# Output projection and the norm behind it joined into one stage by blocks of tokens

## What is computed

```python
h = layer_norm(ALPHA * x + 0.5 * swiglu(x, ...[0]), ln_g[0], ln_b[0])
...   # h @ w_in; retention, forgetting attention and cross-attention, merged by gates g
mix = (g[:, :, 0] * ret_out + g[:, :, 1] * fox_out + g[:, :, 2] * mem_out) @ w_out
h = layer_norm(ALPHA * h + mix, ln_g[1], ln_b[1])
y = layer_norm(ALPHA * h + 0.5 * swiglu(h, w_ffn_gate[1], w_ffn_up[1], w_ffn_down[1]), ln_g[2], ln_b[2])
```

## Time and profile before

| | |
|---|---|
| median of 3 runs | 3609.65 us (3609.44 to 3610.64) |
| the profiled execution | 3616.08 us, span of the core 3614.3 us |
| mean granted TensorE clock | 0.952 of full |
| TensorE matmuls busy | 3295.3 us, 91% of the span |
| VectorE, ScalarE, GpSimd busy | 911.9, 632.3, 792.8 us |
| first load of `w_out` issued | 2565.34 us after the span's start |
| first matmul of the projection | 2577.50 |
| first matmul of the norm | 2681.60 |
| first matmul of the feed-forward layer behind | 2742.89 |

### The profile page before, as it was taken

One profiled execution on the slowest core, in us unless ns is written; L12 is line 12 of the kernel. 1 busy time (PEld: TensorE's weight loads), 2 busy tenths in 40 slices (PEclk: granted clock), 3 DMA queues, 4 the chain that ended last, 5 costly groups with the idle time before them and its releaser, 6 DMA issues. The chain is left out here.

```text
span 3614.3 us, 55597 instructions
## 1 busy us (share of the span) xinstructions
PE 3295.3 (91%) x21001; PEld 2981.3 (82%) x21001; DVE 911.9 (25%) x1606; ACT 632.3 (17%) x1179; POOL 792.8 (22%) x696
## 2 busy tenths in 40 slices
PE   5999999998797898788999899999796999999996
PEld 5999999997796798555888666666686999999995
DVE  3111111113406231555110122222323111111114
ACT  3000000001201111344100244444113000000003
POOL 0232322333120121022111111111021323232220
PEclk7999999999898899899999999999798999999998
DMA  5111111110101211211111499999201111111111
GB/s 144 32 53 37 46 46 35 52 47 24 34 25 38 58 41 56 83 57 48 36 53 38 141 307 291 300 304 302 74 23 35 41 38 49 35 49 49 33 38 54
DMA packets 328683, 293.37 MB, mean 81 GB/s; under 512 B 33641, under 2 KB 249065, under 8 KB 328049
## 3 DMA queue, kind: packets, MB, share of 16 engines
q1 hardware_dynamic: 317136, 275.93, 24.5%
q0 software_dynamic: 11424, 15.76, 1.6%
HBM read 279.34 MB, written 12.26 MB: 81 GB/s over the span
## 5 line engine op out<-in xcount | busy, mean ns | idle before, releaser
L207 PE MATMUL f_acc<-x_hi,w_hi_last 128*128 128x364 f32 x1056 | 233.3, 329 | 27.4 <-SPq L489 27.4
L165 POOL CAST w_hi_first<-w_raw_first 128x1024 fp32r<-128x1024 f32 (+1 forms) x96 | 82.7, 862 | 741.2 <-issue 301.4
L207 PE MATMUL f_acc<-x_hi,w_hi_first 128*128 128x364 f32 x1056 | 233.5, 329 | 6.9 <-SPq L489 6.9
L207 PE MATMUL f_acc<-x_hi,w_lo_first 128*128 128x364 f32 x1056 | 234.2, 330 | 0.0
L207 PE MATMUL f_acc<-x_lo,w_hi_first 128*128 128x364 f32 x1056 | 234.0, 330 | 0.0
L207 PE MATMUL f_acc<-x_hi,w_lo_last 128*128 128x364 f32 x1056 | 233.9, 330 | 0.0
L207 PE MATMUL f_acc<-x_lo,w_hi_last 128*128 128x364 f32 x1056 | 233.5, 329 | 0.0
L165 POOL CAST w_hi_last<-w_raw_last 128x1024 fp32r<-128x1024 f32 (+2 forms) x92 | 73.3, 797 | 612.4 <-PE f_acc L207 608.5
L596 DVE SCALAR_TENSOR_TENSOR br<-f_acc,br 128x1092 f32 x88 | 114.0, 1296 | 368.8 <-PE f_acc L207 368.8
L207 PEld LDWEIGHTS f_acc<-x_hi,w_hi_last 128*128 128x128 f32 x1056 | 183.9, 189 | 28.0 <-issue 28.0
L207 PEld LDWEIGHTS f_acc<-x_hi,w_hi_first 128*128 128x128 f32 x1056 | 184.0, 189 | 7.1 <-issue 7.1
(11 more groups left out here) (402 smaller groups left out, 6322.1 us busy)
## 6 DMA issues: line engine op xcount, KB each, us to landing
br<-cache_fox_k SPq DMA_DIRECT2D x256, 256.0 KB, 5.4
br<-cache_fox_v SPq DMA_DIRECT2D x256, 256.0 KB, 6.6
w_raw_first<-w_ffn_gate SPq DMA_DIRECT2D x22, 512.0 KB, 3.8
w_raw_first<-w_ffn_up SPq DMA_DIRECT2D x22, 512.0 KB, 3.8
w_raw_last<-w_ffn_gate SPq DMA_DIRECT2D x22, 512.0 KB, 3.9
w_raw_last<-w_ffn_up SPq DMA_DIRECT2D x22, 512.0 KB, 3.8
w_raw_first<-w_ffn_down SPq DMA_DIRECT2D x40, 256.0 KB, 2.8
w_raw_last<-w_ffn_down SPq DMA_DIRECT2D x40, 256.0 KB, 2.8
```

The costliest lines, as they stand in the source:

```text
L165: self.nc.gpsimd.tensor_copy(hi, raw).then_inc(self.high[s], 1)
L207: mm = self.nc.tensor.matmul(out[:, b, 0:width], w[s][:, k, :], x[:, k, b * width:(b + 1) * width], start=(k == 0 and first), stop=(k == k ...
```

## The change

`phase_out` and `phase_norm(1)` become one stage, `phase_out_norm`. The tokens are cut into blocks of 416, 416 and 260 columns. The work of the projection is 24 units, each one output tile for one block (24 matmuls, one PSUM bank out of a ring of six). Tiles 0 and 1 run together over the three blocks, then tiles 2 and 3, then tiles 4 to 7 block by block. Weights have four slots for the parts and two for the raw tiles, which lie in rows 8 and 9 of `g.br`. The parts of `mix` are made by quarters: block 0 in two halves of the channels, then block 1, then block 2. The norm is that of the class `Norm`, its steps set between units by hand: the mean of block 0 behind unit 17, its variances behind unit 19, and so on. Squares go into `mix`, the reciprocals into `mem_kt` and `mem_v`. The order on VectorE and ScalarE is written out. The first weights of the feed-forward layer are loaded at the end of SP's list and no longer split in the norm; ScalarE and VectorE split them at the start of `phase_ffn(1)`.

```diff
@@ phase_ffn
             @block.scalar
             def _(act):
+                if layer == 1:
+                    w.first_high(act, KD)
                 act.preload_act_table(ACT.Silu)
...
             @block.vector
             def _(dve):
+                if layer == 1:
+                    w.first_low(dve, KD)
+
@@ phase_out_norm, in place of phase_out and phase_norm(g, 1)
+    STARTS = [0, 416, 832, TW]
+    BLOCKS, HALF, SLOTS, BANKS = 3, KD // 2, 4, 6
+    UNITS = [(j, b) for pair in range(2) for b in range(BLOCKS) for j in (2 * pair, 2 * pair + 1)] \
+        + [(j, b) for b in range(BLOCKS) for j in range(HALF, KD)]
+    LAST = [1 + max(i for i, unit in enumerate(UNITS) if unit == (j, BLOCKS - 1)) for j in range(KD)]
+        quarters = [(0, slice(0, HALF)), (0, slice(HALF, KD))] + [(b, slice(0, KD)) for b in range(1, BLOCKS)]
...
             @block.sync
             def _(sp):
+                for j in range(KD):
+                    if j >= 2:
+                        sp.wait_ge(low, j - 1)
+                    sp.dma_start(w.raw[j % 2], io["w_out"][:, j * P:(j + 1) * P].rearrange("(k p) c -> p k c", p=P))\
+                        .then_inc(loaded[j % 2], 16)
+                sp.wait_ge(low, KD)
+                w.load_next(sp, w.n, ffn_first(io, 1), KD)
             @block.gpsimd
             def _(pool):
+                n1.constants()
+                def split(j):
+                    pool.wait_ge(loaded[j % 2], 16 * (j // 2 + 1))
+                    if j >= SLOTS:
+                        pool.wait_ge(summed, LAST[j - SLOTS])
+                    nc.gpsimd.tensor_copy(hi[j % SLOTS][:], w.raw[j % 2]).then_inc(high, 1)
+                    pool.wait_ge(high, j + 1)
+                    nc.gpsimd.tensor_tensor(lo[j % SLOTS][:], w.raw[j % 2], hi[j % SLOTS][:].bitcast(F32), ALU.subtract)\
+                        .then_inc(low, 1)
+                pool.wait_ge(low, 2)
+                for j in range(2, KD):
+                    split(j)
+                for b in range(BLOCKS):
+                    pool.wait_ge(added, 3 * HALF + HALF * (b + 1))
+                    n1.add_up(pool, b)
             @block.tensor
             def _(pe):
+                def unit(i):
+                    j, b = UNITS[i]
+                    s = j % SLOTS
+                    pe.wait_ge(low, j + 1)
+                    if i >= BANKS:
+                        pe.wait_ge(added, i - BANKS + 1)
+                    for k in range(KD):
+                        if k % HALF == 0:
+                            pe.wait_ge(mix_low, 1 + k // HALF if b == 0 else b + 2)
+                        for x, (wt, src) in enumerate(((hi, g.xh), (hi, g.xl), (lo, g.xh))):
+                            mm = nc.tensor.matmul(bank[i % BANKS][:, 0:n1.width(b)], wt[s][:, k, :], src[:, k, n1.cols(b)],
+                                                  start=(k == 0 and x == 0), stop=(k == KD - 1 and x == 2))
+                    mm.then_inc(summed, 1)
+                units(0, 18)
+                n1.means(pe, 0)
+                units(18, 20)
+                n1.variances(pe, 0)
+                units(20, 22)
+                n1.means(pe, 1)
+                units(22, 24)
+                n1.variances(pe, 1)
+                n1.means(pe, 2)
+                n1.variances(pe, 2)
             @block.scalar
             def _(act):
...
+                n1.square(act, 0)
+                n1.deviation(act, 0)
+                n1.shifted(act, 0, g.xh)
+                n1.square(act, 1)
+                n1.deviation(act, 1)
+                n1.shifted(act, 1, g.xh)
+                n1.square(act, 2)
+                n1.deviation(act, 2)
+                n1.shifted(act, 2, g.xh)
+                for b in range(BLOCKS):
+                    scaled_back(b)
             @block.vector
             def _(dve):
...
+                residual(0)
+                residual(1)
+                weight_lows(0)
+                mix_lows(0)
+                mix_lows(1)
+                weight_lows(1)
+                residual(2)
+                mix_lows(2)
+                residual(3)
+                mix_lows(3)
+                dve.wait_ge(resid, 4)
+                adds(0, 19)
+                n1.centre(dve, 0)
+                adds(19, 22)
+                n1.invert(dve, 0)
+                n1.scale(dve, 0)
+                adds(22, 23)
+                n1.centre(dve, 1)
+                adds(23, 24)
+                n1.invert(dve, 1)
+                n1.scale(dve, 1)
+                n1.centre(dve, 2)
+                lows(0)
+                n1.invert(dve, 2)
+                n1.scale(dve, 2)
+                lows(1)
+                lows(2)
```

More of the change, by code:

```diff
@@ L2814, in _, with units @@
+                def units(first, end):
+                    for i in range(first, end):
+                        unit(i)
+                pe.wait_ge(n1.ready, 2)
+                units(0, 18)
[8 more added lines that the diff above has]
+                n1.variances(pe, 2)
             @block.scalar
@@ L2815, in _ @@
             def _(act):
[L2816 to L2819, removed]
+                for j in range(2):
+                    act.wait_ge(loaded[j], 16)
+                    nc.scalar.copy(hi[j][:], w.raw[j]).then_inc(high, 1)
+                    if j == 0:
+                        for q in range(2):
+                            act.wait_ge(resid, q + 1)
+                            nc.scalar.copy(part(g.xh, q), part(mix, q)).then_inc(mix_high, 1)
@@ new lines, in _, with scaled_back @@
+                for q in range(2, 4):
+                    act.wait_ge(resid, q + 1)
+                    nc.scalar.copy(part(g.xh, q), part(mix, q)).then_inc(mix_high, 1)
+                nc.scalar.mul(alpha_b[:], n1.shift, ALPHA).then_inc(alpha_ok, 1)
+                act.wait_ge(alpha_ok, 1)
+                act.wait_ge(n1.ready, 2)
+                def scaled_back(b):
+                    for k in range(KD):
+                        act.wait_ge(low_row, b * KD + k + 1)
+                        row = g.res[:, k, n1.cols(b)]
+                        nc.scalar.activation(row, row, ACT.Identity, bias=alpha_b[:, k:k + 1], scale=ALPHA)
@@ L2824, in _ @@
[L2824 to L2830, removed]
-                                                ALU.subtract).then_inc(low, 1)
@@ L2832, in _, with residual @@
-                with dve.Fori(0, KD // 2) as j:
-                    for s in range(2):
-                        row = g.res[:, j * 2 + s, :]
-                        dve.wait_ge(w.done[s], j + ((b0, b1)[s] + 2))
-                        nc.vector.scalar_tensor_tensor(blocks_of(row), blocks_of(row), ALPHA, acc[s][:, :, 0:TB],
-                                                       ALU.mult, ALU.add).then_inc(free[s], 1)
-        w.n = [b0 + KD // 2, b1 + KD // 2]
+                def residual(q):
+                    nc.vector.tensor_tensor(part(g.res, q), part(g.xh, q).bitcast(F32), part(g.xl, q).bitcast(F32), ALU.add)\
+                        .then_inc(resid, 1)
@@ new lines, in mix_lows, with weight_lows, adds @@
+                def mix_lows(q):
+                    dve.wait_ge(mix_high, q + 1)
+                    nc.vector.tensor_tensor(part(g.xl, q), part(mix, q), part(g.xh, q).bitcast(F32), ALU.subtract)\
+                        .then_inc(mix_low, 1)
+                def weight_lows(j):
+                    dve.wait_ge(high, j + 1)
+                    nc.vector.tensor_tensor(lo[j][:], w.raw[j], hi[j][:].bitcast(F32), ALU.subtract).then_inc(low, 1)
+                def adds(first, end):
+                    for i in range(first, end):
+                        j, b = UNITS[i]
+                        row = g.res[:, j, n1.cols(b)]
+                        dve.wait_ge(summed, i + 1)
+                        nc.vector.scalar_tensor_tensor(row, row, ALPHA, bank[i % BANKS][:, 0:n1.width(b)], ALU.mult, ALU.add)\
+                            .then_inc(added, 1)
```

62 lines of the change are left out of this document (38 added, 24 removed).

## The result

The joined kernel takes 3621.99 us (median of 11 runs, 3614.26 to 3632.72), the kernel before 3613.69 on the same chip (11 runs, 3609.44 to 3618.65). The ratio is 1.0022, 95% interval 1.0011 to 1.0032: 8 us slower, between 4 and 11.6. The forecast was +0.07%, 3612.3 us, with a range of 3604.5 to 3617.5; the measured time lies above it.

What follows compares the result with a forecast made beforehand. Only the 177.55 us from first load to first feed-forward matmul could move, with ScalarE's last pass ending the stage. Joined stage 0.0, semaphore clearing +0.8, weight split +1.9: +2.7 on 3609.65 gives 3612.3 us, range 3604.5 to 3617.5.

Steps and rivals of the forecast that it cites:

- Part 1, the start: Start of the joined stage: first matmul 9.1 us after the first load instead of 12.2, a gain of 3.1 us.
- Part 2, contention: Before unit 2: GpSimd's splits hold VectorE's sum, charged 2.4 us; unit 2 starts at 24.9 after a 4.4 us stall.
- Part 3, the run of units: Projection units after unit 2: 86.7 us, a 3.0 us wait for block 0's squares, clock losses; last unit ends at 121.8.
- the clock's two losses of 1.8: TensorE's clock falls after the stalls of 4.4 and 3.0 us, costing 1.8 us each (bounds 0 and 2.3).
- Part 4, the tail: Behind the projection: nearly two and a half norms in sequence, then three alpha scalings; ScalarE ends at 175.7 us, gaining nothing.
- Part 5, the boundary: Into the feed-forward: more semaphores to clear, +0.8 us, and first weights split at that stage's start, +1.9 us.
- the prices: The forecast's unit costs, taken from trace rows, for VectorE and ScalarE passes, projection matmuls and norm matmuls at each clock.
- The price of the means: Means of blocks 0 and 1, set among the projection units on TensorE: 0.36 us each.
- (a): Rival: same schedule, VectorE not held (2.4 us) and clock unharmed by stalls (3.6): -3.3 us, 3606.3 us; chance 0.22.
- (b): Rival: the tail also stays at full clock, saving 2.6 and 1.7 us more: -7.6 us, 3602.0 us; chance 0.05.
- (c): Rival: full overlap, only block 2 and scalings behind the last unit, some 30 us: 3588.6 us; chance 0.04.
- (d): Rival: reading the projection's straight code slows each matmul, up to 30 ns for 576, 17 us: 3629 us; chance 0.07.

Runs made afterwards that it cites:

- half_var: The changed kernel with four variance matmuls per block instead of eight: stage 176.1 us against 183.0, ratio to the kernel before 1.0006.
- warm: The changed kernel with never-read matmuls (36 and 58) on TensorE ahead of the variances of blocks 1 and 2: stage 181.0 us, tail 49.2, ratio to before 1.0017.
- best: The changed kernel with tail reordered, alpha passes moved into the feed-forward, unit 20 and block 0's inverse and scaling earlier: stage 156.2 us, ratio to before 0.9934.
- back_later: The changed kernel with the alpha passes over the residual moved to the start of the second feed-forward: stage 179.4 us, ratio to before 1.0001.
- after_again: The changed kernel run once more, unchanged, beside the kernel before: stage 181.5 us, ratio to before 1.0023.

## Why the prediction was wrong

Of the 9.7 us between 3612.3 and 3621.99, 4.0 are the base: the sum stood on the median of three runs, 3609.65, and the kernel before lies at 3612.9 to 3614.0 in 11 to 29 runs. The other 5.6 are the ratio. The stage was forecast at 177.55 + 2.7 = 180.2 and measured at 183.0 and 181.5, which is 2.8 and 1.3 of them; for the rest no run shows a cause. By its steps, in the first profile (zero at the first load):

- **Part 1, the start.** First matmul at 9.7, forecast 9.1, before 12.2: right but for the load, which landed after 5.1 us instead of 4.4.
- **Part 2, contention.** Wrong in its object. VectorE's sum of 3328 columns was forecast at 6 us and took 3.62; GpSimd was the one held, since it started second. What VectorE lost was 0.2 us in its low part for block 1 (3.83 against 3.63) and, not on the way to unit 2, 0.8 in its sum for block 2 (3.16 against 2.32). Unit 2 started at 23.1 instead of 24.9, its wait being 2.41 us instead of 4.4.
- **Part 3, the run of units.** The last ended at 121.3, forecast 121.8, before 113.7 (119.7 in the second profile). The wait for the squares was 2.80 (3.0). The near hit is three errors that cancel: unit 2 earlier by 1.8, the clock's two losses of 1.8 smaller (some 1.5 in all in the first profile, behind unit 2's wait, none in the second), against 3.0 too little for the variances and 0.7 for the means.
- **Part 4, the tail.** The order was read rightly, link by link: from the addition of unit 21 to the scaling of block 0 7.3 us (7.4 forecast), and root to scaling of block 1, 8.1 us as forecast, and shifting and squaring 7.2 and 6.2 (7.4 and 6.4). The two variances failed: 7.3 us instead of 5.5, and 6.3 instead of 3.5. With 1.0 us that the units were ahead and 0.7 saved on ScalarE's passes, the alpha passes end at 178.6 instead of 175.7. That before they "ran mostly between other passes" is misread: two of the three ran at the end there (2732.86 and 2737.04), which the sum, going by ends, did not need.
- **Part 5, the boundary.** 2.05 us to the next stage's first instruction (2.0 forecast) and 2.36 to its first matmul (2.54): right.

**The failed step** is one line of the prices: "Eight of 416 are 2.89 us at the full and 5.5 at the low clock, eight of 260 are 1.8 and 3.5". The row behind it has sixteen records in 5.06 us, and a block's variances are eight matmuls in the code, but sixteen records in the trace. I priced eight records. (At the low clock I took some 0.6 us a record of 364 columns, where the row has nine in 4.5 us at 0.58; half_var's eight of 416 took 5.79 at 0.51.) At 5.8 and 3.7 us for whole blocks at the full clock and 7.3 and 6.3 as met, the stage would have been forecast 7.6 us longer (3.0 + 1.8 + 2.8), at 187.8, and the other errors would have stood out; half_var and the tail's rows show the term. The count stood in the same row: x16. The price of the means, 0.36 instead of 0.7 us each, fails by the same miscount.

The rivals: (a) was wrong in sign, though half its reasons were right: VectorE's sum was not held, and the clock held through some of the pauses. (b) fell, the tail's clock was 0.69 and 0.50; warm puts its price at 3.9 us, forecast 4.3. (c), the full overlap, fell for the change, but describes what the order could give: best is at 156.2, where (c) had 156.2 for the stage (180.2 - 24). That these agree to the tenth is chance, since best also has the alpha passes moved, and (c)'s own terms add up to 28.6 us, not the 30 that it goes on with. (d), slow straight code, fell: TensorE's idle time in the 111.44 us is the two waits (5.21 us) and none lies within units, and the widths cost what was forecast.

The forecast called the order of the tail the reason that nothing is gained. That is shown: with it changed, and nothing else, 13 us of the stage go. What the stage's forecast missed was the price of the variances, not the order.

## What to carry to other kernels

When a stage is cut into blocks so that one block's chain runs under another's matmuls, write out each engine's order behind the last matmul and ask of every instruction ahead of the next link whether that link needs it; here five steps moved (one on TensorE, two on ScalarE, two on VectorE) were worth 13 us, where joining the stages had cost 5. Work that nothing near needs (the scaling of the residual) belongs behind the boundary. Price a group by the records that its row counts, and look up how many records one instruction of the program leaves, before a count from the code is multiplied with a mean from the trace.

## What the runs showed of the hardware

**VectorE and GpSimd take turns by whole instructions,** whoever comes first, when VectorE has two operands in SBUF: a GpSimd cast of 1024 columns with one operand took 4.38 us beside VectorE's 3.62 us sum, and 1.04 alone; VectorE's sum of 2080 columns took 3.16 behind a cast and 2.32 alone; GpSimd's subtraction behind that sum took 4.35, and 2.40 alone. An addition of VectorE out of PSUM (2608.61, 0.42 us in the change) beside such a subtraction (2606.96, 2.40 us) held nobody. Read so, the row of before agrees: of its 2.13 us, 0.98 lie beside GpSimd's instruction and 1.15 behind it, near the 1.291 of the undisturbed one. The Trainium skill, "GPSIMD Engine Reference", section 8. Key points, speaks of contention with VectorE instructions that have two SBUF inputs; the traces agree, for a GpSimd cast with one input (4.38 us against 1.04) as for its subtraction with two.

**A pause of one length, two outcomes.** 2.80 us without matmuls were followed by a granted clock of 0.50 in back_later and of 1.00 in after_again, at the same place of the same code: 8.86 or 5.86 us for the same sixteen records.

**A matmul with float32 operands leaves two records,** for 416 columns at the full clock 0.35 us apart (their weight loads stand at 2672.62, 2672.97 and 2673.32, and sixteen take 5.86 us with the end of the last), while the projection's matmuls of the same width, on parts rounded to fp32r, follow each other at 190 ns (2588.69, 2588.88 and 2589.07 in the timeline of the change).
